# SSD state and scan stage: small matmuls spread over row groups of the array, value products reordered by column half

## The reference, cut to what matters

```
def _ssd_scan(x, dt, a, bm, cm, s0):          # prompt: chunked; sample: one token
    ...
        cum = jnp.cumsum(dtc * a, axis=1)
        decay = jnp.exp(jnp.where(causal, cum[:, :, None] - cum[:, None, :], -jnp.inf))
        cb = jnp.einsum('btgn,bsgn->btsg', cc, bc)
        w = cb[..., None] * decay * dtc[:, None]
        y = (jnp.einsum('btsgh,bsghp->btghp', w, xc)
             + jnp.einsum('btgn,bghpn->btghp', cc, s) * jnp.exp(cum)[..., None])
        s_new = (jnp.exp(last)[..., None, None] * s
                 + jnp.einsum('bsgn,bsgh,bsghp->bghpn', bc, dtc * jnp.exp(last[:, None] - cum), xc))
```

## Time and profile before

| | us |
|---|---|
| median of 3 runs (2770.29 to 2782.28) | 2775.6 |
| the profiled execution: time | 2772.84 |
| the profiled execution: span from first to last instruction | 2770.9 |
| TensorE busy | 2522.1 (91%) |
| VectorE busy | 1295.9 (47%) |
| ScalarE busy | 738.8 (27%) |
| scan block, first to last matmul of it | 1566.9 to 1726.1 |
| mean granted TensorE clock | 0.911 of full speed |

### The profile page before, as it was taken

How to read it: one execution, slowest core, us unless ns; L and a number is a source line. 1 busy time by engine, 2 the same in 40 slices (tenths; PEclk the granted TensorE clock), 3 DMA queues, 4 the chain that set the end, 5 groups by cost and what they waited for, 6 DMA issues and landing times. The chain is left out here.

```text
span 2770.9 us, 45348 instructions
## 1 busy us (share of the span) xinstructions
PE 2522.1 (91%) x18752; PEld 2045.6 (74%) x18752; DVE 1295.9 (47%) x2638; ACT 738.8 (27%) x2055; POOL 0.2 (0%) x4
## 2 busy tenths in 40 slices
PE   5799988889999877999999997889999998888998
PEld 4555566489987665999788766789986556646997
DVE  1215345255642472655442376155651543534665
ACT  0124454221011233210232342222011444622210
POOL 0000000000000000000000000000000000000000
PEclk9899978999999977999999756899999997799999
DMA  9968322967643414667333233467748852084541
GB/s 343 332 202 170 85 86 73 307 228 264 253 153 122 122 37 158 249 243 264 133 122 123 63 107 91 154 231 260 260 162 229 172 130 86 1 255 171 183 153 47
DMA packets 287199, 472.83 MB, mean 171 GB/s; under 512 B 14940, under 2 KB 105005, under 8 KB 286390
## 3 DMA queue, kind: packets, MB, share of 16 engines
q1 hardware_dynamic: 273332, 457.08, 50.8%
q10 hardware_dynamic: 13664, 12.87, 1.5%
HBM read 448.86 MB, written 38.04 MB: 176 GB/s over the span
## 5 line engine op out<-in xcount | busy, mean ns | idle before, releaser
L785 PE MATMUL PS<-hT,ring 128*128 128x132 f32 x2048 | 257.3, 282 | 14.0 <-ACT hT L688 11.9
L785 PEld LDWEIGHTS PS<-hT,ring 128*128 128x128 f32 x2048 | 245.2, 195 | 20.4 <-issue 19.9
L1446 DVE COPY arena<-PS 64x128 f32<-64x128 f32 (+1 forms) x576 | 135.0, 268 | 172.6 <-PE PS L1373 167.9
L785 PE MATMUL PS<-mT,arena 128*128 128x132 f32 x1536 | 186.8, 277 | 0.0
L785 PEld LDWEIGHTS PS<-mT,arena 128*128 128x128 f32 x1536 | 180.8, 192 | 0.0
L2577 PE MATMUL PS<-hT,ring 128*128 128x264 f32 x768 | 174.3, 389 | 2.9 <-DVE hT L667 2.9
L1463 ACT ACTIVATE arena<-PS 64x128 f32<-64x128 f32 (+1 forms) x576 | 125.0, 260 | 166.7 <-PE PS L1373 162.5
L2577 PEld LDWEIGHTS PS<-hT,ring 128*128 128x128 f32 x768 | 146.3, 192 | 28.2 <-issue 3.3
L922 DVE TENSOR_TENSOR arena<-arena,PS 128x264 f32<-128x264 f32 x224 | 90.0, 427 | 135.5 <-PE PS L785 134.3
L1421 PE MATMUL PS<-arena,hT 128*128 128x504 f32 (+1 forms) x320 | 128.6, 554 | 0.0
L785 PE MATMUL PS<-arena,ring 128*128 128x132 f32 x1024 | 127.5, 278 | 0.0
(11 more groups left out here) (444 smaller groups left out, 4160.4 us busy)
## 6 DMA issues: line engine op xcount, KB each, us to landing
arena<-in_w_ada SPq DMA_DIRECT2D x36, 2048.0 KB, 12.2
ring<-in_w_mlp_in SPq DMA_DIRECT2D x32, 2048.0 KB, 8.4
ring<-in_w_mlp_out SPq DMA_DIRECT2D x32, 2048.0 KB, 8.5
ring<-in_w_ada SPq DMA_DIRECT2D x12, 2048.0 KB, 19.4
ring<-in_ssd_w_in SPq DMA_DIRECT2D x12, 2048.0 KB, 8.1
ring<-in_nsa_w_in SPq DMA_DIRECT2D x10, 2048.0 KB, 22.1
arena<-in_cache_nsa_kv SPq DMA_DIRECT2D x64, 256.0 KB, 8.8
ring<-in_cache_nsa_kv SPq DMA_DIRECT2D x64, 256.0 KB, 8.5
```

Of the source, the lines that this page charges most:

```text
L785: ins = nc.tensor.matmul(PS[:, bank, at:at + HALF], lhs[:, k, p * 128:(p + 1) * 128], rhs[:, k, :], start=opens and k == 0, stop=closes an ...
L1446: ins = nc.vector.tensor_copy(dst, src)
```

## The change

In the scan block, the operands of the small matmuls are laid out in different groups of 32 partitions. The outer products of half a sample's heads alternate between partitions 0 to 7 and 32 to 39, and write bank 4 and bank 5 in turn. The C row is read from partitions 64 to 71. The four broadcasts of `cum` alternate between partitions 0 to 31 and 32 to 63, where ScalarE has made a copy (`cum_low`), and banks 1 and 2. The eight value products of a group are issued so that the two heads of a pair, which lie in different column halves, take turns. The number and the sizes of the matmuls stay as they are. Copies that fill these layouts are split in two: L2745 (for B), L2920 and L2940.

```
+            cum_low = arena[32:64, cum_at:cum_at + SEQ]
...
                         nc.scalar.activation(dec[:, SEQ:T], cum[:, SEQ:T], ACT.Exp)
+                        nc.scalar.activation(cum_low, cum[:, 0:SEQ], ACT.Copy)
...
-                bc_tok = P(2 * SSD_G * SSD_N, rows=NB)
+                group_rows = P(SSD_G * SSD_N)
+                b_rows = [group_rows[32 * y:32 * y + NB, 0:512] for y in range(2)]
+                c_rows = group_rows[64:64 + NB, :]
...
-                dxT = halves[4][0:NB]
+                dxT = [halves[4][32 * y:32 * y + NB, 0:1024] for y in range(2)]
...
+                            elif n < 14:
+                                for y in range(2):
+                                    ins = nc.vector.tensor_copy(b_rows[y][:, (n - 12) * 256:(n - 11) * 256],
+                                                                PS[0:NB, n % 4, 256 * y:256 * y + 256])
                             else:
-                                ins = nc.vector.tensor_copy(bc_tok[:, (n - 12) * 512:(n - 11) * 512], PS[0:NB, n % 4, :])
+                                ins = nc.vector.tensor_copy(c_rows[:, (n - 14) * 512:(n - 13) * 512], PS[0:NB, n % 4, :])
...
-                masked = [hT_flat[0:NB, 1024 + 512 * h:1536 + 512 * h] for h in range(2)]
+                masked = [[hT_flat[32 * y:32 * y + NB, 1024 + 256 * h:1280 + 256 * h] for y in range(2)] for h in range(2)]
...
-                            for h in range(4):
+                            for h in (0, 2, 1, 3):
+                                r = 32 * (h // 2)
                                 ins = nc.tensor.matmul(PS[:, 1 + h // 2, (h % 2) * SEQ:(h % 2 + 1) * SEQ],
-                                                       ident[0:32, 4 * g + h:4 * g + h + 1].broadcast_to([32, 128]),
-                                                       cum[:, 0:SEQ], start=True, stop=True)
+                                                       ident[r:r + 32, r + 4 * g + h:r + 4 * g + h + 1].broadcast_to([32, 128]),
+                                                       (cum_low if r else cum[:, 0:SEQ]), start=True, stop=True)
...
-                            for i in range(8):
-                                j = 8 * h + i
-                                ins = nc.tensor.matmul(PS[:, 4 + i // 4, (i % 4) * 128:(i % 4 + 1) * 128],
-                                                       dxT[:, j * 128:(j + 1) * 128],
-                                                       masked[h][:, (i // 2) * 128:(i // 2 + 1) * 128], start=True, stop=True)
+                            for i in range(4):
+                                for y in range(2):
+                                    ins = nc.tensor.matmul(PS[:, 4 + y, i * 128:(i + 1) * 128],
+                                                           dxT[y][:, 512 * h + i * 128:512 * h + (i + 1) * 128],
+                                                           masked[h][y][:, (i // 2) * 128:(i // 2 + 1) * 128],
+                                                           start=True, stop=True)
...
-                            c_ready.on(nc.tensor.matmul(PS[:, 6, :], ident[0:NB, b:b + 1].broadcast_to([NB, 128]),
-                                                        bc_tok[:, 1024 + 512 * h:1536 + 512 * h], start=True, stop=True))
+                            c_ready.on(nc.tensor.matmul(PS[:, 6, :], ident[64:64 + NB, 64 + b:65 + b].broadcast_to([NB, 128]),
+                                                        c_rows[:, 512 * h:512 * h + 512], start=True, stop=True))
...
-                            for h in range(4):
-                                hh = slice((4 * g + h) * 64, (4 * g + h + 1) * 64)
-                                o = PS[64 * (h % 2):64 * (h % 2) + 64, 3 + 4 * (g % 2), (h // 2) * SEQ:(h // 2 + 1) * SEQ]
-                                nc.tensor.matmul(o, xdt[:, 0, hh], W[g % 2][:, h, 0:SEQ], start=True, stop=False)
-                                ins = nc.tensor.matmul(o[:, 128:SEQ], xdt[:, 1, hh], W[g % 2][:, h, SEQ:384],
-                                                       start=False, stop=True)
+                            for pair in range(2):
+                                for i, (t0, w0, w1) in enumerate(((0, 0, SEQ), (128, SEQ, 384))):
+                                    for e in range(2):
+                                        h = 2 * pair + e
+                                        ins = nc.tensor.matmul(
+                                            PS[64 * e:64 * e + 64, 3 + 4 * (g % 2), pair * SEQ + t0:(pair + 1) * SEQ],
+                                            xdt[:, i, (4 * g + h) * 64:(4 * g + h + 1) * 64], W[g % 2][:, h, w0:w1],
+                                            start=i == 0, stop=i == 1)
...
-                            mask_ready.on(nc.scalar.activation(masked[h], bc_tok[:, 512 * h:512 * h + 512], ACT.Copy,
-                                                               scale=ident[0:NB, b:b + 1]))
+                            for y in range(2):
+                                ins = nc.scalar.activation(masked[h][y], b_rows[y][:, 256 * h:256 * h + 256], ACT.Copy,
+                                                           scale=ident[32 * y:32 * y + NB, 32 * y + b:32 * y + b + 1])
+                            mask_ready.on(ins)
...
-                            dx_moved.on(nc.scalar.activation(dxT[:, 1024 * r:1024 * r + 1024].rearrange("p (x n) -> p x n", x=2),
-                                                             PS[0:NB, 4 + 2 * r:6 + 2 * r, :], ACT.Copy))
+                            for y in range(2):
+                                ins = nc.scalar.activation(dxT[y][:, 512 * r:512 * r + 512], PS[0:NB, 4 + 2 * r + y, :], ACT.Copy)
+                            dx_moved.on(ins)
```

More of the change, by code:

```diff
@@ L2535, in mixer_ssd @@
             dt = P(T, rows=32)
+            cum_at = P.at
             cum = P(T, rows=32)
+            cum_low = arena[32:64, cum_at:cum_at + SEQ]
             dec = P(T, rows=32)
```

## The result

| | before | after |
|---|---|---|
| median, us | 2778.94 (4 runs, 2770.29 to 2785.77) | 2749.97 (4 runs, 2738.84 to 2753.71) |
| ratio, 95% interval | | 0.9891 [0.9849, 0.9932] |
| span of the profiled execution, us | 2770.9 | 2748.0 |

The changed kernel is 1.1% faster, 29.0 us by the medians.

The account below looks back on a forecast made before the run. TensorE was taken to set the scan block's period, VectorE next. Gains 5.3 + 24.1 + 1.0 - 0.3 = 30.1 us take 2772.84 to 2742.7; 2.8 for the median gives 2745.5, stated as 2745, range 2737 to 2758 (likeliest case 2740 to 2751).

Parts of the forecast that it names:

- copies in the turn block: Before the scan block, two of four L2745 copies become pairs of 8x256 on VectorE: 0.3 us lost, bounds 0 to 1.2.
- start, to the second L2896 or L2908: Start of the scan block: the second product of weights and scores comes at 1591.1 for 1596.39 us, gain 5.3.
- six periods: Scan block between the second and eighth L2896: 105.06 us becomes 6 x 13.5 = 81.0, gain 24.1.
- end, to L2908 or L2920: End of the scan block: the wait of 1.04 us for the last outer products goes, gain 1.0.
- what follows: After the periods, last state and last store: same work, no change taken, -2 to +5 us kept for the range.
- VectorE becomes the bound, at 13.4 a period: Scan block periods: VectorE's own work, 13.4 us, replaces TensorE's as what sets the period; 13.5 was used.
- The outer products just in time: Scan block period: last outer product ready at 15.05 us after L2896 starts, wanted by the next L2881 at 15.2.
- Row groups of 32 overlap as the halves in the earlier trace do: TensorE in the scan block: two matmuls in the time of one; outer products 3.42 to 1.71 us, broadcasts 3.57 to 1.87.
- Value products: nothing: Value products in the scan block: column halves already run side by side, so the new order gains nothing; still 2.82 us.
- C row beside the outer products: Scan block: the C row's 1.84 us run beside the outer products; if behind, period 13.9, 2748 us, chance 0.18.
- about 10: TensorE's work per scan block period, in us at 1.2 GHz, if the C row overlaps the outer products; 13.5 if not.
- Clock: TensorE idles in each period and may stay at 1.2 GHz all along; figures assume that clock, so no cost.

Follow-up runs that it names:

- unloading VectorE: The changed kernel without the reductions L2901 for samples 1 to 7, their y left out; four inner periods of 12.14 to 12.15 us.
- turns of four: The changed kernel with four outer products of the first row group issued, then four of the second; first period 13.30 us, the other five 14.39 or 14.40.
- the repeat: The changed kernel run once more, unaltered; median 2745.7 us, ratio 0.9877, scan block 132.8 us.
- the kernel with the longer periods: The changed kernel with the C row read from partitions 0 to 7, the first row group; 2733.2 us, six periods in 83.57 us.

## Why the prediction was right

By its own terms, the first column as predicted, the second from the stretches above:

| term | predicted | measured |
|---|---|---|
| copies in the turn block | -0.3 | -0.55 (11.90 to 12.45) |
| start, to the second L2896 or L2908 | 5.3 | 5.68 (29.49 to 23.81) |
| six periods | 24.1 | 24.66 (105.06 to 80.40) |
| end, to L2908 or L2920 | 1.0 | 0.71 (11.24 to 10.53) |
| what follows | 0 | -1.45 (19.64 to 21.09) |
| sum | 30.1 | 29.05 |

- **VectorE becomes the bound, at 13.4 a period.** Right: 13.40 in each, VectorE busy for 13.02 of it, no wait left. (The sum went by 13.5, with 0.1 for what just misses.) This was the step on which most of the sum stood, and unloading VectorE confirms it.
- **The outer products just in time.** Right, and shown from the other side: turns of four make them 1.0 us longer, and the period grows by 1.0.
- **Row groups of 32 overlap as the halves in the earlier trace rows do.** Right for both kinds: 3.62 to 1.92 us for the outer products, 3.78 to 2.08 for the broadcasts. By single starts two outer passes begin 0.006 us apart.
- **Value products: nothing.** Right, by the kernel with that edit alone (0.05 us). The Trainium skill's statement that matmuls keep program order in start and end (TensorE: Matmul & The Clock Gate, "The mechanism") does not hold here for the starts: the C row's first pass starts before six outer passes that stand ahead of it in the program, 1610.17 against 1610.37. The ends in the trace are modelled and say nothing on it.
- **C row beside the outer products.** Right in what it does to the period, and only partly in how: it does not start with them but 0.87 us later, four pass times. TensorE's total of "about 10" was too low, since about 1 us of the C row stands behind the outer products each time (1611.22 to 1612.24), twice a period; it is busy for 12.17 us of the period from 1622.87 us, which is all at 1.2 GHz. No term stood on it.
- **End.** 0.71 for 1.0: the wait for the last outer products fell from 1.04 to 0.33 and did not go. The sixteen passes took 2.08 us there (1681.04 to 1683.12) at a clock of 0.50, and 2.05 in the kernel before (1706.77 to 1708.82) at 1.00: the higher clock had already given what the two groups give.
- **Copies.** Mis-sized: four copies of 8x256 take 1.70 us on VectorE where two of 8x512 take 1.28, so 0.42 and not 0.3, still within the bounds given; the turn block as a whole is 0.55 longer.
- **Clock.** I took it as costing nothing. Inside the periods that is right: they are 13.40 us with a mean of 0.63 and with 0.50. After them it is not: L2853 takes 10.33 us for 8.88, at a mean of 0.66 for 0.76 over its stretch. This lay inside the stated -2 to +5. And the start depends on it: to the first product of weights and scores 10.68 us at 0.66 in this profile and 8.18 at 0.86 in the repeat, for 12.71 at 0.50 before. By the repeat the start's gain would be 8.2 us and not 5.68. So it is in part luck that the start came within 0.4 us of the prediction and the whole sum within about 1. What holds in both profiles is the 24.66 of the periods.

The gain of the turn and scan blocks by the profiles is 29.05 us and that of the spans 22.9. The 6.2 us between stand outside the block, 4.8 ahead of the turn block and 1.3 behind, where the code is the same but for one ScalarE copy. The repeat of the changed kernel shows this to be spread: its scan block begins at 1580.83 us, 8.6 later than in the first profile. The medians are 29.0 us apart in the first set of runs and 32.1 in the set of the repeat; the scan block alone is 29.6 us shorter in the first profile (165.4 to 135.8) and 32.6 in the repeat.

## What to carry to other kernels

Where matmuls contract over few rows, put neighbours in different groups of 32 partitions and issue them in strict turns (here they also wrote different banks, and whether that is needed was not measured); before reordering anything by column halves, look whether the trace has them side by side already. Count the new bound before the gain: at 1.2 GHz the broadcasts alone took 1.7 us off TensorE's work in a period and the period fell by 1.7 (18.64 to 16.93); the outer products alone took 3.4 off it, and the period fell by 3.1 (to 15.51), because a loop of waits took over; with all parts it fell by 5.2 (to 13.40), where VectorE took over. Set the gain against what ran before at the clock it had: the six periods of the kernel before had a mean of 17.51 us, not 18.64, as some of TensorE's work ran at 2.4 GHz, so the same three steps gave 0.6, 2.1 and 4.1 us a period. When an engine is relieved, follow each loop of waits around once at the new durations; here that gave 13.4 and, with VectorE relieved too, 12.0, and both were measured to within 0.2 us.

## What the runs showed of the hardware beyond that

- A row group that is free starts a matmul from further on in the program, but not from any distance: the C row started 0.87 us (four passes) after the outer products ahead of it, and the second group of turns of four 0.86 us late.
- TensorE may be busy without a break and still be granted 1.2 GHz: 101.56 us of 101.56 in the kernel with the broadcasts alone, clock 0.50. The kernel before had matmuls of the same number and sizes and a mean of 0.56 over the same six periods. So 5.5 of 9 us of gain on paper did not come.
- The same instructions ahead of the block take up to 15 us more or less from one execution to the next: the scan block began at 1572.26 us in the first profile of the changed kernel, at 1580.83 in the repeat and at 1565.97 in the kernel with the C row in the first group, though the code ahead of both is the same but for where one buffer lies. Their total times alone (2733.2 for the kernel with the longer periods) would have ranked them wrongly.
